# The start of a long kernel put in another order: memory norm ahead, weight splits shared by two engines, state-space tables on one engine

## The reference, cut to what matters

```python
h = rms_norm(x, norm1_g)                       # x: 1024 tokens x 1024
q, k, v, g_ret, u, g_s5 = split(h @ w_in)
ret = retention(q, k, v) * silu(g_ret)
ssm = s5_branch(u, a, dt, b, c, d, ...) * silu(g_s5)
x = x + concat([ret, ssm]) @ w_out
m = rms_norm(mem, norm_mem_g)                  # 256 memory tokens
ka, va = m @ xa_wk, m @ xa_wv                  # keys and values of the cross attention
x = x + cross_attention(rms_norm(x, norm2_g) @ xa_wq, ka, va) @ xa_wo
x = second_block(rms_norm(x, norm_f_g))        # mixers and a feed-forward part, not touched
```

## Time and profile before

| | us |
|---|---|
| median of 3 runs | 2873.59 (2866.3 to 2878.86) |
| the profiled execution, its own time | 2872.58 |
| its span, first to last instruction | 2870.8 |
| start to the first unit of `u` on PE | 115.75 |
| two groups of table transposes on PE, up to the next unit | 139.74 to 140.53 |
| multiplication of one table slice on PE, up to the next unit | 152.56 to 156.77 |
| first transposes of `s5_in` on PE | 264.82 |
| scan on DVE | 385.95 to 600.94 |
| end of the last unit of `gs5` on PE | 613.56 |

### The profile page before, as it was taken

The page is one execution under the profiler, slowest core; times in us unless marked ns, Lnnn a source line. Parts: engine busy times, 40 slices in busy tenths (PEclk is TensorE's granted clock), DMA queues, the critical chain, the costliest instruction groups (busy, mean ns, idle before and its releaser), DMA issues.

```text
span 2870.8 us, 36466 instructions
## 1 busy us (share of the span) xinstructions
PE 2585.6 (90%) x15202; PEld 2128.1 (74%) x15202; DVE 1156.4 (40%) x1950; ACT 572.2 (20%) x901; POOL 701.6 (24%) x323
## 2 busy tenths in 40 slices
PE   6799999969799899969989789787889999999998
PEld 5588888857677678858777677566668888888887
DVE  7790258731578534022512151554232222222223
ACT  4111112102312012122323223444021000000002
POOL 2584313230022123210311210000322222233330
PEclk9899999989899999989999998888889999999999
DMA  7455433244245471431142341112311111111101
GB/s 245 129 169 162 132 121 108 77 132 132 82 142 175 143 244 46 160 117 67 60 146 76 111 152 65 46 32 70 119 44 45 44 44 44 44 44 50 58 30 59
DMA packets 225844, 284.64 MB, mean 99 GB/s; under 512 B 30801, under 2 KB 143410, under 8 KB 225714
## 3 DMA queue, kind: packets, MB, share of 16 engines
q1 hardware_dynamic: 193458, 234.41, 25.5%
q10 hardware_dynamic: 32256, 48.35, 4.6%
HBM read 200.83 MB, written 81.89 MB: 98 GB/s over the span
## 4 chain that ended last, share of the span: by engine, by line
PE 78%; DVE 10%; ACT 3%; DMA 3%; POOL 3%; issue 2%; SPq 1%; ACTq 0%; DVEq 0%; POOLq 0%
PE PS L460 22%; PE PS L2861 17%; PE PS L463 14%; PE PS L2878 8%; PE PS L1240 2%; POOL W_LO L426 1%; PE PS L1238 1%; PE PS L1580 1%; PE PS L1778 1%; PE PS L637 1%; PE PS L1579 1%; PE PS L1798 1%; DVE T L923 1%; DVE T L924 1%; PE PS L2307 1%
## 5 line engine op out<-in xcount | busy, mean ns | idle before, releaser
L420 POOL TENSOR_SCALAR W_HI<-RAW 128x2048 fp32r<-128x2048 f32 (+1 forms) x66 | 132.9, 2015 | 1495.1 <-PE PS L460 580.8
L460 PE MATMUL PS<-W_HI,OP_HI 128*128 128x512 f32 (+1 forms) x1184 | 308.1, 404 | 19.2 <-issue 9.2
L460 PE MATMUL PS<-W_LO,OP_HI 128*128 128x512 f32 (+1 forms) x1184 | 288.5, 386 | 0.0
L460 PE MATMUL PS<-W_HI,OP_LO 128*128 128x512 f32 (+1 forms) x1184 | 286.4, 384 | 0.0
L426 POOL TENSOR_TENSOR W_LO<-RAW,W_HI 128x2048 fp32r<-128x2048 f32 (+1 forms) x59 | 272.3, 4616 | 44.5 <-DVE W_LO L406 39.9
L460 PEld LDWEIGHTS PS<-W_HI,OP_HI 128*128 128x128 f32 x1184 | 222.9, 196 | 66.9 <-issue 14.9
L460 PEld LDWEIGHTS PS<-W_LO,OP_HI 128*128 128x128 f32 x1184 | 221.4, 190 | 45.4
L460 PEld LDWEIGHTS PS<-W_HI,OP_LO 128*128 128x128 f32 x1184 | 219.0, 188 | 43.7
L463 PE MATMUL PS<-OP_HI,W_HI 128*128 128x512 f32 (+1 forms) x768 | 196.1, 399 | 19.2 <-DVE OP_LO L1269 12.4
L484 ACT ACTIVATE OST<-PS 128x512 f32<-128x512 f32 (+2 forms) x164 | 94.6, 577 | 538.9 <-PE PS L463 271.5
L2861 PE MATMUL PS<-OP_HI,W_HI 128*128 128x512 f32 x704 | 176.0, 392 | 14.0 <-POOL W_LO L2843 14.0
(11 more groups left out here) (422 smaller groups left out, 3661.9 us busy)
## 6 DMA issues: line engine op xcount, KB each, us to landing
RAW<-in_w_in SPq DMA_DIRECT2D x28, 1024.0 KB, 5.2
RAW<-in_w_gate_up SPq DMA_DIRECT2D x44, 512.0 KB, 4.7
RAW<-in_w_out SPq DMA_DIRECT2D x12, 1024.0 KB, 7.2
RAWD<-in_w_down SPq DMA_DIRECT2D x11, 1024.0 KB, 4.9
x_d<-X SPq DMA_DIRECT2D x2, 4096.0 KB, 16.1
X<-x_d SPq DMA_DIRECT2D x2, 4096.0 KB, 13.8
ptok_d<-OST ACTq DMA_DIRECT2D x24, 256.0 KB, 2.0
pch_d<-OST ACTq DMA_DIRECT2D x24, 256.0 KB, 2.0
```

The costliest lines, as they stand in the source:

```text
L420: nc.gpsimd.tensor_scalar(hi, raw, 1.0, 1.0, ALU.mult, ALU.mult).then_inc(*w_hi.by(1))
L460: ins = nc.tensor.matmul(PS[:, bank, 0:width], act_part[:, k, (g.tile0 + a) * P:(g.tile0 + a + 1) * P], w_part[:, slot, k, 0:width], start ...
```

## The change

- `dve_first` and `act_first`: the parameters stand no longer ahead of the memory norm on DVE; a root of a constant at the start loads ACT's table for roots.
- `DVE_HALVES` goes from (0, 1, 2, 3, 4, 6, 8) to (0, 2, 4, 6, 8): POOL also subtracts halves 1 and 3.
- All tiles of x are transposed in the stretch of `xk` and `xv` (before, tile 7 came after the output matrix was read out); norm tiles are due earlier and 3.8 apart instead of 3.6.
- The parameters come late: their transposes and that of the output matrix stand behind the first unit of `u` on PE; on DVE the first part of the formulas comes ahead of the last low part of x, the squarings behind the last weight half of the start.
- `pool_s5_tables` is gone; DVE makes each slice of the output table behind that slice of the input table (`outputs`). PE and SP have the slices due earlier (`bt_time` 2.5 + 3.2 per slice instead of 3.6 + 3.7), and `s5_in` as well (1.9 instead of 4.8 units behind the 16 units of `u`).

```diff
-    DVE_HALVES = (0, 1, 2, 3, 4, 6, 8)
+    DVE_HALVES = (0, 2, 4, 6, 8)
...
-        return 3.6 + 3.7 * (n // 4) + (0.0, 0.05, 1.0, 1.05)[n % 4]
+        return 2.5 + 3.2 * (n // 4) + (0.0, 0.05, 1.0, 1.05)[n % 4]
...
-        yield 18
+        yield 50.5
+        dve.wait_ge(*xn_full(turned_base(1) + 5))
+        V.memset(CPB[:, :, :, :, :], 0.0).then_inc(*s5_rsb.by(1))
+        yield 51
         dve.wait_ge(*s5_act(4))
         tt(w(14), w(11), w(13), MUL)
...
-        yield 28
+        yield 55
         re, im = 14, 15
         for k in range(3):
...
+        def outputs(i):
+            pairs = slice_pairs(i)
...
+            src = CP[:, :, pairs, :]
+            for n in range(SC):
+                chain(V.tensor_tensor(T12[:, 0], src, spread(0), MUL))
+                chain(V.tensor_tensor(T12[:, 1], src, spread(6), MUL))
+                V.tensor_tensor(CPW[:, 0, :, n, :], T12[:, 0, 0], T12[:, 1, 1], SUB).then_inc(*s5_cpw.by(1))
+                V.tensor_tensor(CPW[:, 1, :, n, :], T12[:, 0, 1], T12[:, 1, 0], ADD).then_inc(*s5_cpw.by(1))
+                dve.wait_ge(*s5_cpw(2 * (SC * i + n + 1)))
+                src = CPW[:, :, :, n, :]
...
             if i >= 1:
                 read_back(i - 1)
+            outputs(i)
         read_back(NSL - 1)
...
-        for t in range(TT - 2):
-            yield 28 + 3.6 * t
+        for t in range(TT):
+            yield NORM_START + NORM_TILE * (t + 3.2) + 1.5
             pe_turn(pe, 1, t)
-        yield 48
+
+    def pe_s5_tables(pe):
+        T = nc.tensor
+        yield 0.4
         pe.wait_ge(*s5_small(4))
...
     def s5_in_time(m):
-        return 4.8 + 1.05 * m
+        return 1.9 + 1.05 * m
...
-            pool_split(pool, 0, 10)
-            pool_s5_tables(pool, 0)
-            pool_split(pool, 10, 12)
-            pool_s5_tables(pool, 1)
-            pool_split(pool, 12, 14)
-            pool_s5_tables(pool, 2)
-            pool_s5_tables(pool, 3)
-            pool_split(pool, 14, len(halves))
+            pool_split(pool, 0, len(halves))
             pool_ffn(pool)
```

More of the change, by code:

```diff
@@ L83 @@
         "la_in0 nx_in0 16,la_in1 nx_in1 16,la_in2 nx_in2 16,la_in3 nx_in3 16,s5b_in s5_bt_out1 128,"
-        "g_gn s5_cpw 128,rt_out s5_zero_out 112,xi_in0 s5_in 144,xi_in1 s5_dd 4,xi_out0 s5_out 256,"
+        "g_gn s5_cpw 64,rt_out s5_zero_out 112,xi_in0 s5_in 144,xi_in1 s5_dd 4,xi_out0 s5_out 256,"
         "xi_out1 s5_bt_out 128").split(",")):
@@ L739, in build @@
     S5_LOADED = 16 * 9
-    XK_START, XK_UNIT, XV_START, XV_UNIT = 18.0, 2.95, 42.0, 5.5
+    XK_START, XK_UNIT, XV_START, XV_UNIT = 18.0, 2.95, 41.8, 5.5
+    NORM_START, NORM_TILE = 10.8, 3.8
     def w(k):
@@ L788, in sp_s5_tables @@
         outs = [(bt_time(n) + 0.8, n, None) for n in range(2 * SLP)]
-        outs += [(time, None, i) for i, time in enumerate((3.0, 9.0, 14.8, 18.8))]
+        outs += [(time, None, i) for i, time in enumerate((4.2, 7.4, 10.6, 13.8))]
         for time, n, i in sorted(outs, key=lambda x: x[0]):
@@ L820, in dve_first @@
         for t in range(2):
-            yield 6.8
+            yield 6.8 + t
             dve_norm_var(dve, 0, t)
-        for t in range(2):
-            yield 7.6 + t
             dve_norm_recip(dve, 0, chain, t)
@@ L877, in dve_s5_params @@
         V.tensor_copy(w(4), w(im)).then_inc(*s5_small.by(1))
[L878 to L881, removed]
+        yield 59
+        dve.wait_ge(*xn_full(turned_base(1) + TT))
+        V.memset(ZER[:, :], 0.0).then_inc(*s5_rsb.by(1))
+        yield 68
         dve.wait_ge(*s5_prm_t(1))
@@ L930, in dve_s5_tables @@
                 read_back(i - 1)
+            outputs(i)
         read_back(NSL - 1)
[L933 to L956, removed]
     def act_first(act):
+        yield 2
+        act.wait_ge(*s5_small(1))
+        act.activation(st[:, 63:64], halfpi[:, :], ACT.Sqrt)
         yield 5
@@ L2972, in _ @@
             sp_first(sp)
-            together(paced(sp_weights_steps(sp, 2 * gemms["gret"].first_block + 4, gemms["u"].first_block), 4, 1),
+            together(paced(sp_weights_steps(sp, 2 * gemms["gret"].first_block + 4, gemms["u"].first_block), 2.5, 1),
                      sp_s5_tables(sp), later(2 * TT, sp_s5_in(sp)))
@@ L3031, in _ @@
             together(act_first(act), act_s5_params(act),
-                     paced(act_norm_tiles(act, 1, 0, lambda t: nx_in[t // 2](16), free={TT - 2: mm_done(gemms["xv"].end)}), 15, 3.6),
+                     paced(act_norm_tiles(act, 1, 0, lambda t: nx_in[t // 2](16), free={TT - 2: mm_done(gemms["xv"].end)}), NORM_START, NORM_TILE),
                      paced(act_gemm_store_steps(act, "xk", lambda b, a, h, w: ka_d[(4 * b + a) * P:(4 * b + a + 1) * P, :]),
@@ L3063, in _ @@
             together(dve_first(dve, chain), dve_s5_params(dve, chain), dve_s5_tables(dve, chain),
-                     dve_split_first(dve, (12.2, 15.2, 22, 25, 34, 46, 58)),
-                     paced(dve_norm_tiles(dve, 1, chain, 0), 15, 3.6))
+                     dve_split_first(dve, (9, 21.6, 31.5, 43.5, 54.5)),
+                     paced(dve_norm_tiles(dve, 1, chain, 0), NORM_START, NORM_TILE))
             dve_s5_in(dve)
```

48 lines of the change are left out of this document (20 added, 28 removed).

## The result

The changed kernel is slower by 0.9%: median 2898.36 (2890.21 to 2902.83, 4 runs) against 2871.03 (2866.3 to 2878.86, 4 runs) of the kernel before, ratio 1.0089, 95% interval 1.0056 to 1.0122. The forecast was 2898. The profiled execution took 2902.83, 4.5 above its own median, so its trace shows some 3 more than the medians' 27.3.

A forecast was written before the change was run, and what follows sets the result against it. PE, busy for 90% of the span, was taken as the bound, with DVE's tables setting its waits. An earlier `u` (-4.7) and late table slices (+30) gave +25 on 2872.58, so 2898; range 2864 to 2910.

The forecast's parts named there:

- Term 1: Prologue up to the start of `u` on PE: begins at 111.0 instead of 115.75, -4.7.
- the walk keeps the lead of `xk`: Prologue, changed order walked with trace durations: `xk` begins some 2.9 sooner, and `xv` ends at 93.5 instead of 96.67.
- Term 2: Input table slice 0 on DVE: held up by a weight block on POOL, ready at U+34; PE waits 14.
- U: Start of `u` on PE, 115.75 in the kernel before, forecast at 111.0.
- Term 3: Slices 1 to 3: PE waits 10 at slice 2 only; `s5_in` late by about 30, Term 2 included.
- the sum to slice 2: DVE's work behind U until slice 2: 11 + 3 x 11.6 + 2 x 13 + 2 x 11.6 = U+95, wherever the blocks fall.
- the sum of 11 ahead of slice 0: Start of the table stage: squarings, zero memset, parameters and diagonal done by U+11, before slice 0's table steps.
- The sum: Whole kernel: -4.7 + 30 = +25 against the profiled 2872.58, so 2898.
- The scan stayed hidden: Scan beside PE's work up to `gs5`: ended 12.6 ahead before; both move by at most 30, so it stays hidden.
- The rule weighed: Output table's engine: VectorE by operation count, 1.45 a step against 2.23 on POOL; forecast no gain, PE waits for input table.
- Partly missed hold-up: Rival on the table slices: DVE held up less, excess of 5 to 18, 2873 to 2886, say 2876; chance 0.23.
- far sooner `u`: Rival on the norm of x's tiles: scalings not held up, `u` at 99, 2861 or 2856; chance 0.13.

The follow-up runs named there:

- e3: Changed kernel with the memset of `CPB` and the 15 formula operations in DVE's idle time before the low part of tile 6; 2892.78.
- e9: Kernel before with memory's norm first and the parameter work put off to places between the tiles; 2877.02.
- e10: Changed kernel with the low parts of weight halves 1 and 3 back on DVE; 2892.60.
- e7: Changed kernel with output table on POOL, due times of before, formulas and squarings in DVE's idle time, parameter and output matrix transposes ahead of `u`; 2869.20.
- e8: e7 with the low part of weight half 8 also in DVE's idle time; 2855.38.
- e4: Changed kernel with weight half 10 on POOL held until slice 0 of the input table is done; 2897.26.
- e2: Kernel before with only the output table moved to DVE and the due times of the changed kernel; 2891.15.
- e12: e8's prologue with the output table on DVE and the due times of the changed kernel; 2883.64.
- e6: Changed kernel with POOL filling weight halves 10 to 13 by memsets instead of splitting them, those products left out (good for time only); 2874.73.
- e1: Changed kernel with the table stage of before: output table on POOL, due times of before; 2874.25.

## Why the prediction was right

**Term 1** was forecast as -4.7 and measured as -5.8: `xk` 23.27 for "near 23.2", end of `xv` 92.24 for 93.5, then 17.7 for 17.5. e3 confirms the 6 for memset and formulas. But one step of its reasoning holds only for the whole change: that the walk keeps the lead of `xk`. e9 shows that memory's norm first does not carry its lead to `u` when the parameter work lies between the tiles. That the lead lives in the changed kernel because that work was put off further is likely, but not shown alone: e9 also keeps the tiles' due times of before, and only the share of the weight halves was tried separately (e10). The work need not be late for it: in e7 and e8 it stands in DVE's idle time, and `u` begins sooner still.

**Term 2**: slice 0 at U+34 forecast, U+32.9 measured; wait 14 and 13.4; half 10 at U+18 to U+20, in fact U+18.3.

**Term 3**: no wait at slice 1, right. Slice 2 at U+95 with a wait of 10 was forecast, U+92.5 with 7.5 measured. Behind slice 0, DVE had slice 2 ready after 59.6 instead of 60.8, and PE came for it after 52.1 instead of 50.8. The forecast of PE's side was right by two errors that cancel: it takes the 3 for the slow clock twice although it has no wait at slice 1, for by its own terms PE comes after 25.4 + 22.2 = 47.6; and PE on the way took 27.8 and 24.3 instead of 25.4 and 22.2, since rows ran slow not only behind the wait but also behind the multiplications (3.76 and 3.45 for the first rows of the next unit, instead of 2.07). The first transposes of `s5_in` at U+168, in fact U+165.9. That the sum to slice 2 holds "wherever the two blocks fall" is shown by e4 (93.1) and e3 (93.6). With parameters early, the sum of 11 ahead of slice 0 goes: e2 and e12 have U+83.5 and U+84.4. The size of the hold-up, 2 x 11.6, stands in DVE's rows (23.0 and 23.3 for a slice beside a block, 11.5 for one without), and e6 shows that it goes with POOL's reads: slice 2 comes 92.5 - 71.5 = 21.0 sooner there, and PE, no longer DVE, sets the pace.

**The sum**: +30 behind U forecast, 28.9 measured at the end of `gs5`. There the trace is late by 23.1, where 25 was forecast; both terms were off by 1.1 to the slow side. Over the whole span the traces differ by 30.2, so 7.1 arise behind `gs5`, where nothing was changed, and 5.8 of these in one place, where the execution of the kernel before alone had the higher clock (last section). The medians say 27.3, and their interval reaches from 16 to 35, so neither figure contradicts the sum. The hit of 2898 to within 1 us is therefore luck: the mechanism and the terms are right to a few us, and the rest is what such a measurement can't resolve. The forecast holds that the earlier due times let nothing start sooner, which is so; that they may cost up to 13, by the estimate above, it does not weigh. The scan stayed hidden: the wait for `URy` is 24.3, against 24.9 before.

**The rule weighed.** By operations VectorE is the better place for the output table; e1 against the changed kernel, and e12 against e8, show the move, with its due times, to cost 24 and 28 (27 and 28 by the ratios to the kernel before of each group). PE waits for the input table, and the output table in front of it on the same engine delays it whatever its own speed.

**The rivals.** Partly missed hold-up (2876) and far sooner `u` did not occur; e6 shows that the first would have given about its time, 2874.73.

## What to carry to other kernels

Before moving work to the faster engine, write down what then stands ahead of the result that the bound engine waits for, and add the other engine's instructions that will hold it up; if the sum exceeds the slack, moving the collision helps nothing (e4). Give the bound engine other work ahead of what comes late, rather than less; the due times here did the opposite, though what that costs was not measured. Look for idle time ahead of the critical stretch first: the memset, formulas, squarings and one low part, placed where DVE waited for the end of `xv`, with the transposes that follow from them ahead of `u`, are all that tells e8 from e1, and gave 19 us (17 against the kernel before). A lead won early survives only up to the next wait that something else ends (e9, e1).

## What the runs showed of the hardware

**A memset on POOL did not hold DVE up**, see e6: 1.81 for 128x2048, with DVE's rows at their usual 0.42 and 0.29 beside it.

**Short operations against short ones.** Beside POOL's own table steps, one DVE step takes 2.54 instead of 1.45; in e8, first DVE, then two rows of POOL that begin a step each:

```profile
106.74 0.64 DVE L921 TENSOR_TENSOR T<-XPWa,PRM 128x256 f32<-128x256 f32 x1
107.42 0.57 DVE L922 TENSOR_TENSOR T<-XPWa,PRM 128x256 f32<-128x256 f32 x1
108.02 0.60 DVE L923 TENSOR_TENSOR XPWa<-T 128x128 f32<-128x128 f32 x1
108.54 0.71 DVE L924 TENSOR_TENSOR XPWa<-T 128x128 f32<-128x128 f32 x1
109.28 0.64 DVE L921 TENSOR_TENSOR T<-XPWa,PRM 128x256 f32<-128x256 f32 x1
```

```profile
107.78 0.69 POOL L948 TENSOR_TENSOR T<-CPW,PRM 128x256 f32<-128x256 f32 x1
...
110.32 0.69 POOL L948 TENSOR_TENSOR T<-CPW,PRM 128x256 f32<-128x256 f32 x1
```

The rows of both engines begin in turn, one of each, and both take 2.54 for a step: DVE instead of 1.45, POOL instead of 2.23. A table of eight steps then takes 20 on DVE, which before fitted in front of PE.

**The granted clock of a stretch differs between executions.** The first row behind `gs5` stands at 638.51 in the kernel before and at 638.40 in e6, with the same code behind it. Yet 300 us later the windows read, for the kernel before and then for e6:

```profile
938.51:968.51 30.00, 25.90 (x139) 20.70 (x140) 17.85 (x42) 2.29 (x3) 0.00 (x0) 0.89 0.39 131
```

```profile
938.40:968.40 30.00, 26.02 (x103) 20.27 (x104) 14.51 (x39) 2.29 (x3) 0.00 (x0) 0.66 0.34 107
```

The clock was 0.89 of full speed in one and 0.66 in the other, and in 30 us the one got through 36 more matmul instructions. In both, PE had just waited (7.50 and 7.21) and then ran small matmuls; the small rows of the kernel before are fast from 946.35 on (0.48), those of e6 stay slow (0.79) to their end at 955.5. The same work, from the transposes behind the wait to the next ones, took 15.8 in the kernel before (942.61 to 958.37) and 21.8 in e6 (942.38 to 964.18). In the other twelve executions profiled here, the changed kernel's among them, it took 21.3 to 22.5, at whatever time it came, with a clock of 0.63 to 0.68 in the same window. Which of the two levels, 1.2 or 2.4 GHz, is granted there is thus worth some 6 us of one trace against another, though e6 had made it up by the end of the span (2870.7 and 2870.8). A comparison of single traces behind `gs5` can't be finer than that.
